# MLP of a hybrid decoder trunk, chunks 2 to 7: the high weight slice meets the high and the low rows in one matmul of 512 columns

## The reference, cut to what matters

```python
z = rms_norm(x, ln2_g[layer]) @ w_up[layer]          # x: (256, 1024), w_up: (1024, 4096)
x = x + jnp.square(jax.nn.relu(z)) @ w_down[layer]   # w_down: (4096, 1024)
```

## Time and profile before

| what | value |
|---|---|
| time, median of 3 runs | 702.62 us (699.68 to 703.37) |
| the profiled execution's own time | 698.07 us |
| its span, first to last instruction | 696.3 us |
| TensorE busy in the span | 634.0 us (91%) |
| VectorE, ScalarE, GpSimd busy | 452.4, 360.5, 229.4 us |
| mean granted TensorE clock | 0.970 of 2.4 GHz |

### The profile page before, as it was taken

How to read it: one execution, slowest core, us unless ns; L and a number is a source line. 1 busy time by engine, 2 the same in 40 slices (tenths; PEclk the granted TensorE clock), 3 DMA queues, 4 the chain that set the end, 5 groups by cost and what they waited for, 6 DMA issues and landing times.

```text
span 696.3 us, 11359 instructions
## 1 busy us (share of the span) xinstructions
PE 634.0 (91%) x4308; PEld 545.7 (78%) x4308; DVE 452.4 (65%) x822; ACT 360.5 (52%) x666; POOL 229.4 (33%) x391
## 2 busy tenths in 40 slices
PE   5968787689899999999999999689989999999995
PEld 4847655478899889988978787457789998999884
DVE  7699488736655569596547778873756455545554
ACT  5744357573654653444436646874455445444451
POOL 6899124640404599980002401582000000000001
PEclk9999998899999999999999999998999999999998
DMA  9474421204685555637546840221545666566641
GB/s 271 144 184 110 123 43 32 78 31 121 185 258 194 165 182 185 217 109 248 173 120 202 220 138 2 46 62 39 160 147 201 207 186 184 176 199 196 183 123 60
DMA packets 60401, 102.77 MB, mean 148 GB/s; under 512 B 18057, under 2 KB 24186, under 8 KB 60314
## 3 DMA queue, kind: packets, MB, share of 16 engines
q1 hardware_dynamic: 55642, 97.65, 46.5%
q0 software_dynamic: 1248, 2.69, 1.7%
q10 hardware_dynamic: 3456, 1.70, 0.9%
HBM read 99.66 MB, written 1.31 MB: 145 GB/s over the span
## 4 chain that ended last, share of the span: by engine, by line
PE 70%; DVE 16%; issue 5%; POOL 3%; ACT 2%; SPq 2%; DMA 2%; DVEq 0%; POOLq 0%; ACTq 0%
PE pb L1690 68%; DVE w_lo L1253 4%; DVE sc_zone L1583 1%; DVE x L1182 1%; SPq L558 1%; DVE dtmp L1175 1%; DVE ca L1175 1%; DMA raw<-in_w_in 1%; DVE dtmp L1450 1%; PE pb L2073 1%; POOL dtmp L777 1%; PE pb L1820 1%; DVE h_lo L1182 1%; DVE top L1446 1%; ACT w_hi L835 1%
## 5 line engine op out<-in xcount | busy, mean ns | idle before, releaser
L1253 DVE TENSOR_TENSOR w_lo<-raw,w_hi 128x1024 fp32r<-128x1024 f32 (+2 forms) x176 | 229.0, 1317 | 137.7 <-ACT w_hi L835 137.3
L835 ACT ACTIVATE w_hi<-raw 128x1024 fp32r<-128x1024 f32 (+2 forms) x184 | 187.7, 1027 | 224.2 <-PE pb L1690 199.9
L1690 PE MATMUL pb<-h_hi,w_hi 128*128 128x256 f32 x512 | 146.0, 285 | 2.5 <-DVE h_lo L1182 1.8
L1690 PE MATMUL pb<-h_hi,w_lo 128*128 128x256 f32 x512 | 145.6, 284 | 0.0
L1690 PE MATMUL pb<-h_lo,w_hi 128*128 128x256 f32 x512 | 145.5, 284 | 0.0
L1690 PEld LDWEIGHTS pb<-h_hi,w_hi 128*128 128x128 f32 x512 | 99.0, 193 | 4.1 <-DVE w_lo L1253 3.0
L1690 PE MATMUL pb<-w_hi,z_hi 128*128 128x512 f32 x256 | 99.9, 390 | 0.4 <-DVE w_lo L1253 0.4
L1690 PE MATMUL pb<-w_hi,z_lo 128*128 128x512 f32 x256 | 99.8, 390 | 0.0
L1690 PE MATMUL pb<-w_lo,z_hi 128*128 128x512 f32 x256 | 99.6, 389 | 0.0
L1690 PEld LDWEIGHTS pb<-h_hi,w_lo 128*128 128x128 f32 x512 | 99.0, 193 | 0.4
L1690 PEld LDWEIGHTS pb<-h_lo,w_hi 128*128 128x128 f32 x512 | 98.9, 193 | 0.0
(11 more groups left out here) (305 smaller groups left out, 877.2 us busy)
## 6 DMA issues: line engine op xcount, KB each, us to landing
raw<-in_w_up SPq DMA_DIRECT2D x64, 512.0 KB, 4.4
raw<-in_w_down SPq DMA_DIRECT2D x64, 512.0 KB, 4.3
raw<-in_w_in SPq DMA_DIRECT2D x24, 512.0 KB, 4.5
raw<-in_w_out SPq DMA_DIRECT2D x8, 512.0 KB, 3.7
raw<-in_w_out SPq DMA_DIRECT2D x16, 256.0 KB, 3.9
raw<-in_w_in SPq DMA_DIRECT2D x8, 308.0 KB, 3.1
raw<-in_w_in SPq DMA_DIRECT2D x8, 280.0 KB, 2.9
x<-in_x ACTq DMA_DIRECT2D x4, 256.0 KB, 4.2
```

Source lines behind the costliest of these rows:

```text
L835: hi_made.by(act.activation(w_hi[:, n % RING, 0:width(n)], raw[:, n % RING, 0:width(n)], ACT.Copy))
L1253: lo_made.by(dve.tensor_tensor(w_lo[:, n % RING, 0:width(n)], raw[:, n % RING, 0:width(n)], w_hi[:, n % RING, 0:width(n)].bitcast(F32), AL ...
L1690: return pe.matmul(o, l, r, start=start, stop=stop, skip_group_check=True)
```

## The change

For chunks 2 to 7, `h_hi` and `h_lo` become the two halves of one tensor `h`, side by side for each k, so that one matmul with the high weights streams both, 512 columns, into a whole bank: high x high falls into its left half and high x low into its right half. The low weights follow with the high rows alone, 256 columns, into the left half. A chunk now takes the four banks `pb0` to `pb3`, one for each f. Chunks 0 and 1 keep `mm3`.

ScalarE copies the four right halves to `z_low` (128 x 256 each); VectorE adds the left halves to them, giving `z_sum` (four adds); ScalarE then does the ReLU in place (one instruction of 1024 columns instead of two of 512 out of PSUM). The square moves from VectorE to ScalarE for all chunks. VectorE's `z_lo` subtraction moves from the end of `square(c)` to behind the second `lo` of the next chunk (for chunk 7: behind the first `lo` of the last four). up(c) waits for the adds of the chunk before it (up(2): for the ReLU of chunk 1).

```diff
-            h_hi, h_lo, z_hi, z_lo = (split.enter_context(nc.sbuf_tensor(name, shape, F32R)) for name, shape in (
-                ("h_hi", [PART, KB, SEQ]), ("h_lo", [PART, KB, SEQ]),
-                ("z_hi", [PART, 2, 4, SEQ]), ("z_lo", [PART, 2, 4, SEQ])))
+            h, z_hi, z_lo = (split.enter_context(nc.sbuf_tensor(name, shape, F32R)) for name, shape in (
+                ("h", [PART, KB, 2, SEQ]), ("z_hi", [PART, 2, 4, SEQ]), ("z_lo", [PART, 2, 4, SEQ])))
+            h_hi, h_lo = h[:, :, 0, :], h[:, :, 1, :]
...
                     act.wait_ge(used.sem, used.at(L, up_at(c) + 4))
-                    for i in range(2):
-                        m = act.activation(z_relu[:, i * 512:(i + 1) * 512], pb[2 * par + i][:], ACT.Relu)
-                        if i == 0:
-                            step(m, False)
+                    if c < 2:
+                        for i in range(2):
+                            m = act.activation(z_sum[:, i * 512:(i + 1) * 512], pb[2 * c + i][:], ACT.Relu)
+                            if i == 0:
+                                step(m, False)
+                    else:
+                        for f in range(4):
+                            low_sb.by(act.activation(z_low[:, f * SEQ:(f + 1) * SEQ], pb[f][:, SEQ:2 * SEQ], ACT.Copy))
+                        act.wait_ge(z_added.sem, z_added.at(L, c - 1))
+                        m = act.activation(z_sum, z_sum, ACT.Relu)
                     relu_sb.by(m)
+                    act.wait_ge(relu_sb.sem, relu_sb.at(L, c + 1))
+                    if c:
+                        act.wait_ge(zlo_sb.sem, zlo_sb.at(L, c))
+                    zsq_sb.by(act.activation(z_sq, z_sum, ACT.Square))
                     act.wait_ge(zsq_sb.sem, zsq_sb.at(L, c + 1))
                     zhi_sb.by(act.activation(z_hi[:, par].rearrange("p f t -> p (f t)"), z_sq, ACT.Copy))
...
-                def square(c):
+                def added(c):
+
+                    for f in range(4):
+                        dve.wait_ge(low_sb.sem, low_sb.at(L, 4 * (c - 2) + f + 1))
+                        part = slice(f * SEQ, (f + 1) * SEQ)
+                        w = dve.tensor_tensor(z_sum[:, part], pb[f][:, 0:SEQ], z_low[:, part], ALU.add)
+                        if f < 3:
+                            step(w, False)
+                    z_added.by(w)
+
+                def low_part(c):
+
                     par = c % 2
-                    if c:
-                        dve.wait_ge(zlo_sb.sem, zlo_sb.at(L, c))
-                    dve.wait_ge(relu_sb.sem, relu_sb.at(L, c + 1))
-                    zsq_sb.by(dve.tensor_tensor(z_sq, z_relu, z_relu, ALU.mult))
                     dve.wait_ge(zhi_sb.sem, zhi_sb.at(L, c + 1))
                     zlo_sb.by(dve.tensor_tensor(z_lo[:, par].rearrange("p f t -> p (f t)"), z_sq,
                                                 z_hi[:, par].rearrange("p f t -> p (f t)").bitcast(F32), ALU.subtract))
...
-                square(0)
+                low_part(0)
                 for n in range(down_at(0), down_at(0) + 4):
                     lo(n)
-                square(1)
                 for c in range(2, CHUNKS):
                     if L < DEPTH - 1 and c == 3:
                         den(L + 1)
                     for n in range(up_at(c), up_at(c) + 8):
                         lo(n)
-                    square(c)
+                        if n == up_at(c) + 1:
+                            low_part(c - 1)
+                    added(c)
                 for n in range(down_at(CHUNKS - 1), PIECES):
                     lo(n)
+                    if n == down_at(CHUNKS - 1):
+                        low_part(CHUNKS - 1)
...
-                    if c >= 2:
-                        pe.wait_ge(relu_sb.sem, relu_sb.at(L, c - 1))
+                    if c == 2:
+                        pe.wait_ge(relu_sb.sem, relu_sb.at(L, 2))
+                    if c > 2:
+                        pe.wait_ge(z_added.sem, z_added.at(L, c - 2))
...
-                                m = mm3(pb[2 * (c % 2) + f // 2][:, (f % 2) * SEQ:(f % 2 + 1) * SEQ],
-                                        w_hi[:, q, col], w_lo[:, q, col], h_hi[:, k, :], h_lo[:, k, :],
-                                        k == 0 and f % 2 == 0, k == KB - 1)
+                                if c < 2:
+                                    m = mm3(pb[2 * c + f // 2][:, (f % 2) * SEQ:(f % 2 + 1) * SEQ],
+                                            w_hi[:, q, col], w_lo[:, q, col], h_hi[:, k, :], h_lo[:, k, :],
+                                            k == 0 and f % 2 == 0, k == KB - 1)
+                                else:
+                                    mm(pb[f][:], w_hi[:, q, col], h[:, k].rearrange("p a t -> p (a t)"), k == 0, False)
+                                    m = mm(pb[f][:, 0:SEQ], w_lo[:, q, col], h_hi[:, k, :], False, k == KB - 1)
```

More of the change, by code:

```diff
@@ L183, in trunk @@
         projf = proj[:].rearrange("p t n -> p (t n)")
-        z_relu = projf[:, 0:4 * SEQ]
+        z_low = projf[:, 0:4 * SEQ]
         z_sq = projf[:, 4 * SEQ:8 * SEQ]
+        z_sum = projf[:, 8 * SEQ:12 * SEQ]
         o_sq = projf[:, 0:KB * SEQ].rearrange("p (k t) -> p k t", k=KB)
@@ L400, in trunk @@
         relu_sb = sig("relu_sb", CHUNKS)
+        low_sb, z_added = sig("low_sb", 4 * (CHUNKS - 2)), sig("z_added", CHUNKS - 2)
         zsq_sb = sig("zsq_sb", CHUNKS)
```

## The result

The changed kernel takes 706.23 us in the median of 8 runs (703.79 to 707.75). The kernel before, run beside it, takes 700.12 us (8 runs, 697.10 to 703.37). The ratio is 1.0084 with a 95% interval of 1.0054 to 1.0114, some 5.9 us slower. The forecast was +1.0 us and "within 0.5%"; slower by more than 0.5% had a chance of 0.17. The time lies in the range that was given around the earlier median, but the difference is six times the forecast one, so the terms of the sum are gone through one by one here.

The account below looks back on a forecast made before the run. TensorE was taken to bound the MLP, with layer 0 near VectorE's limit. The terms -5.1 -1.4 (old layer 0 loss gone) +2.25 +3.7 +0.75 +0.8 gave +1.0 us on 702.6, so 703.6 us, range 699.0 to 707.5.

Parts of the forecast that it names:

- TensorE's saving: In up(2) to up(7) of both layers, one start fewer per group saves 13.4 ns, 5.1 us in all.
- The chain: From z to the next weights: the next chunk's first `lo` starts at T+8.46, leaving 1.2 us of cover of 3.7.
- The table loads: Chunk 3 of layer 0: two table loads leave little cover, so TensorE stalls for 2.25 us.
- The first burst: Chunk 4 of layer 0: VectorE's `lo` and `z_lo` take turns with GpSimd, so TensorE stalls 3.7 us.
- The second burst: Layer 0, meeting chunk 5 at about 294: the next chunk's first `lo` comes 0.75 us late (0 to 2).
- rival (b): Stalls let TensorE's granted clock fall; two falls give 705.6 us, to 707 if each lasts longer; chance 0.12.
- The adds do not contend: VectorE's adds read one operand from PSUM, so they stay under 0.5 us even beside a GpSimd burst.
- The end of layer 1: Chunk 7: the moved `z_lo` delays the last `lo`, so the last four matmul groups wait 0.8 us longer.

Follow-up runs that it names:

- run 1: The changed kernel with ScalarE making the next chunk's first high piece ahead of its wait for the adds; 697.61 us, ratio 0.9971 to the kernel before.
- run 7: The changed kernel with `z_lo` back in its old place on VectorE, directly behind the adds; 702.22 us, ratio 1.0044 to the kernel before.
- run 3: The changed kernel with TensorE's matmuls ordered four wide, then four narrow; 705.32 us, ratio 1.0081 to the kernel before.
- run 4: The changed kernel with the square back on VectorE, behind the adds; 705.79 us, ratio 1.0104 to the kernel before.

## Why the prediction was right in its mechanism and short in its sum

**TensorE's saving: mis-sized by half.** The step reads "I take 5.1, because both widths have the same 13 ns". Measured are 6.7 ns a group instead of 13.4, and 0.19 us a period, so 2.3 us. The two widths were read in streams of their own, and alternating them costs 6.7 ns more at the wide one. The order of matmuls decides that (periods of 22.23, 22.13 and 22.05 us by pairs, fours and eights; the forecast's saving would give 21.99). The Trainium skill (TensorE: Matmul & The Clock Gate, Back-to-back issue gap) gives a warm matmul its columns over 2.4 GHz plus 2.5 ns, which it calls the gap of an isolated matmul; the estimate from it was 1.0 us, and the trace agrees neither with it nor with this step.

**The chain: right.** First `lo` forecast at T+8.46, measured T+8.16. The adds are 0.33 us apart, not 0.40, and that is most of the 0.3.

**The table loads: right.** 2.25 forecast, 2.1 measured in the period, and it goes when the first piece is made ahead of them (run 1: 22.23).

**The first burst: right in size and place.** 3.7 forecast, 4.1 measured, the third `lo` as named, with `z_lo`'s turn ahead of it. Inside the sum two errors cancel in part: the third `lo` cost about 3.3 us and not 2.55, and the next down did not wait, where 0.6 was forecast. What was wrong came later, in the expectation of run 7: that the place of `z_lo` makes no difference. With it back in its place chunk 4 lost 2.8 us less and chunk 5 0.5 more.

**The second burst: the step that failed.** It reads "0.75 us (0 to 2)" and stands on "The second burst meets chunk 5 at about 294". It began at 289.88. Then all of chunk 5's last `lo` take turns, the last is done at 305.76 and not at 302.8, the adds follow it at 307.1, and TensorE waits 2.17 us, with 1.7 us of slow clock behind: 3.8 in all. I had carried the delay of the first burst over to the second. But GpSimd made up for its late start of 2.2 us: the first burst began at 256.89 and not at 257.7; VectorE was idle then, so two operations took 1.95 and 1.96 us instead of about 2.9; the burst ended at 273.15 (before: 273.71), and the small operations up to the second burst took 16.7 us instead of 18.8. So rival (b), to which 0.12 was given, came true once. Against it the forecast had set that TensorE is full on both sides of such a stall; that did not hold the clock here. Why it fell there, and not behind the longer wait of 3.14 us, no run explains. The other traces only show that the length of the wait does not decide it: in run 3 the clock stayed behind 3.13 us, in run 4 it fell behind 2.09, 2.54 and 3.59 us. It stays open.

**The adds do not contend: right.** All 48 adds last 407 to 418 ns, with the four at 305.68 to 307.08 beside the second burst's last operation (304.63 to 308.02). The `lo` just ahead of them, with two SBUF inputs, lasts 3.41 us:

```profile
L1643 DVE TENSOR_TENSOR proj<-pb,proj x48: 407/416/418, 229.1 to 676.3; 128x256 f32<-128x256 f32 x48
...
302.35 3.41 DVE L1265 TENSOR_TENSOR w_lo<-raw,w_hi 128x1024 fp32r<-128x1024 f32 x1
```

The Trainium skill says that VectorE contends with GpSimd's reads when both of its inputs lie in SBUF, and not when one does (SBUF — State Buffer, Who interferes with whom). This trace agrees, with 3.41 and 0.418 us.

**The end of layer 1:** 0.8 forecast, 0.4 measured.

So the mechanism was the forecast's: TensorE's small gain is paid for with the cover of the next weights. The sum missed 3 us at the second burst and 2.8 at TensorE, and both misses had the same sign; the other terms missed by 0.4 us or less. That the time still fell inside the range is luck of the base: the range stood around an earlier median of 702.6 us, and the kernel before took 700.12 us beside the changed one. As differences the range was -3.6 to +4.9 us, and the measured +5.9 (3.8 to 8.0) lies outside it, though its interval reaches in.

## What to carry to other kernels

When work is added to a chain on an in-order engine, look at what stands behind the chain, not at its consumer: here the next weights, whose copy could stand in the idle time ahead of a wait for 8 us of gain. A moved operation belongs where its engine has nothing ready, even if nobody needs it soon: in run 7 chunk 4 became 2.8 us shorter with `z_lo` in such a place. A delay must be followed through every later meeting with another engine's burst, not shifted along as a constant.

## What the runs showed of the hardware that was not expected

A matmul of 512 columns between matmuls of 256 costs 0.233 us from start to start, against 0.2266 in a stream of its own; with four together about half of the extra is gone, with eight about three quarters (periods from 22.23 to 22.13 to 22.05 us, of a possible 21.99). Why was not tried. The granted clock fell to 1.2 GHz for 3.4 us behind an idle time of 2.17 us (a mean of 0.68 over 5.3 us) and stayed at 2.4 GHz behind one of 3.14 us in the same trace. In run 4's trace it fell behind 2.09, 3.59 and 2.54 us and stayed behind 1.54; each fall cost 1.7 us.

Two operations of 128 x 1024 with two SBUF inputs, one of VectorE and one of GpSimd, took turns of about 2.9 us; alone they took 1.22 and 1.95 us.
